# Attention heads of a hybrid decoder layer: sample rows in array tiles, group weights on turned probabilities, features stored by class

## The chip, the cores and the metric

The program runs on one core of one Trainium2 chip. The metric is the device time of one execution in microseconds (us). TensorE (PE in the profile) multiplies matrices into PSUM, VectorE (DVE), ScalarE (ACT) and GpSimd (POOL) work elementwise, and SyncE (SP) issues most transfers.

## The reference

One layer of a hybrid decoder runs for a prompt of 1024 tokens and for 8 sample sequences of 8 new tokens (64 sample rows). After an RMSNorm one combined projection gives the inputs of three branches: dilated window attention, a gated linear recurrence (HGRN2) and causal pooling. Each branch is gated, projected and merged, and an output projection follows. The attention is the part that changes:

```python
A_PATTERNS = ((128, 1), (512, 4), (2048, 16))      # (window, dilation) of the 3 groups, 4 heads x 128 each
def dilated_attn_sample(q, k_all, v_all, dilation, n_steps):
    idx = (n_ctx - T + jnp.arange(T))[:, None] - dilation * jnp.arange(n_steps + 1)[None, :]
    scores = jnp.einsum('bthe,btjhe->bthj', q, k_all[:, idx_c], ...) * (e ** -0.5)
    scores = jnp.where(valid[None, :, None, :], scores, NEG)
    lse = jax.nn.logsumexp(scores, axis=-1)
    p = jnp.exp(scores - lse[..., None])
    o = jnp.einsum('bthj,btjhe->bthe', p, vg)
...
w_grp = jax.nn.softmax(jnp.stack(lses, axis=0), axis=0)      # weight of each group, per token and head
o_a = jnp.einsum('gblh,gblhe->blhe', w_grp, jnp.stack(outs, axis=0))
y_a = (o_a * jax.nn.silu(ag))
```

For the prompt, token t of a group with dilation d reads keys t - j*d, so tokens fall into residue classes modulo d. The last 128, 512 and 1024 key and value rows of the three groups are outputs too. In the recurrence branch each of 8 heads also has 8 sample states of 128x128, read and updated by the sample rows.

## The kernel before, in words

The program is a sequence of phases: norm, attention (4 heads, one loop turn each), recurrence (`hgrn_phase`, 8 heads), pooling, two merges, output. All share a *conveyor*: a weight tile of 1024x128 is loaded by SP (`cv.load`, two slots), split by POOL into a high and a low part, and projected by PE in three token chunks (384, 384, 320 columns) of 24 matmuls each (`cv.project`, L230). ACT copies every chunk out of PSUM banks 0 to 2. The other PSUM banks form a ring of 3 in attention (banks 3, 4, 7): `cv.fill` lets PE write a ring bank once DVE has copied out the use three before, `cv.filled` lets DVE read it. Uses of the ring are numbered within a head (`M_S`, `M_K`, `M_V`, `M_KT`, ...), and every engine works strictly in its written order.

One attention head projects 10 units: queries and keys of the three groups (units 0 to 5), values (6 to 8) and the gate (9). Unit 0 belongs to the end of the previous turn. PE's order in a turn is: units 1, 2; prompt scores of group 0 (L1350); key rows of group 0 turned from features to rows for the key output (L1361); units 3, 4; the same for group 1; units 5, 6; the same for group 2. Then the cached sample keys, four 128-row blocks for each of the 8 sequences, are turned (`keys_t`, L1386), and the sample scores are made (`key_scores`, L1394) with the keys as the stationary operand and 8 query columns as the moving one. They lie under the chunks of units 7 and 8, together with the value rows (`v_rows`). The scores are copied out by DVE and turned back to rows (L1431). Unit 9 follows, then the sample probabilities are turned, and `sample_values` (L1458) multiplies them with the cached values, in 32 matmuls of 64 columns of probability that are zero outside the own sequence. At last the 35 probability blocks of the prompt are turned four at a time (`turn`, L1473), copied by DVE (L1721), and multiplied with the value rows (`values`, L1483 to L1491).

An fp32 matmul shows as two records in the trace. Features of a token stand in the order of time, so that groups 1 and 2 read them with a step of 4 or 8 elements:

```python
if g == 1:
    r, n = c // 2, c % 2
    return src[:, 4 * P * n + r:4 * P * n + r + 4 * (P - 1) + 1:4]
return src[:, c:c + 8 * (P - 1) + 1:8]
```

The group weights need all three groups' row maxima and sums by token. After ACT's exponentials (`exps(2)`, L1525), SP writes the statistics of groups 1 and 2 to HBM (L1296, L1299), waits for them, reads them back by token (L1303), DVE works out the weights (L1669 to L1684, with one exponential on ACT between), and SP carries them back by class (L1309 to L1317). DVE then scales all 24 pieces of the probabilities (L1704) before PE may turn them (`scaled`).

In `hgrn_phase`, `own_states` (L896 to L904) multiplies the queries of the 64 sample rows with the 8 sample states (8 matmuls, queries zero outside the own sequence) and makes the 8 state updates in two matmuls of 512 columns.

Of the kernel before, what the change touches and what calls it, by code (L numbers as in the profile page):

```python
# [25 lines left out]
F32 = mybir.dt.float32  # L26
F32R = mybir.dt.float32r
I32 = mybir.dt.int32
ALU = mybir.AluOpType
# [4 lines left out]
P = 128  # L34
# [30 lines left out]
def constants(np):  # L65
# [15 lines left out]
    c["level"] = lev  # L81
    j = np.arange(NS)
# [23 lines left out]
def build(nc, A, OUT):  # L106
    ctx = ExitStack()
    with ctx:
# [31 lines left out]
        weight_d = nc.dram_tensor("group_weights", (AH, SEQ, 2), F32, kind="Internal").ap()  # L140
# [544 lines left out]
        def hgrn_phase(ext, p_gate, p_graw, then):  # L685
# [10 lines left out]
            with scope:  # L696
# [71 lines left out]
                with nc.Block() as block:  # L768
# [86 lines left out]
                    def _(pe):  # L855
# [29 lines left out]
                        def own_states(i):  # L885
                            cv.copied(pe, i * MISC, M["k"] + 2)
                            for q in range(2):
                                bank = cv.fill(pe, i * MISC, M["ds"] + q)
                                for b in range(4):
# [7 lines left out]
                                      start=True, stop=False)  # L897
                            for b in range(NB):
                                mm = pe.matmul(bank[0:NS, 0:P], qown[:, b, :], s0[:, b, :],
                                               start=False, stop=(b == NB - 1))  # L900
# [229 lines left out]
        def attention_phase(then):  # L1130
# [7 lines left out]
            UNITS, MISC = 10, 51  # L1138
            KB = 4
            KW = KB * P + AG * NS  # L1140
            K_G = (0, 1, 1, 2)
            scope = ExitStack()
            with scope:
# [25 lines left out]
                wt = sb("a_weight", (P, TILES, 2), F32, scope)  # L1169
                w0 = sb("a_weight0", (P, TILES), F32, scope)  # L1170
                w12 = sb("a_weight12", (P, 2, TILES), F32, scope)
                yt = graw

                kv = [sb(f"s_cached{i}", (P, KB, P), F32, scope) for i in range(NB + 4)]
                VC = [8, 9, 10, 11, 0, 1, 2, 3]
                mask = sb("s_mask", (NS, KW), F32, scope)
                qh = sb("s_q", (P, AG, NS), F32, scope)
                kh = sb("s_k", (P, AG, NS), F32, scope)
                kt = [sb(f"s_k_feature{i}", (P, KB, P), F32, scope) for i in range(2)]
                sct = sb("s_scores_t", (P, KB, NS), F32, scope)  # L1180
# [5 lines left out]
                orow = sb("s_o_rows", (NS, P), F32, scope)  # L1186
                s_rows_ready = sem("s_rows_ready", scope)
                s_turned = sem("s_turned", scope)
# [8 lines left out]
                s_scores_out = sem("s_scores_copied", scope)  # L1197
# [6 lines left out]
                scores_max = sem("a_negmax_ready", scope)  # L1204
                exp_done = sem("a_exp_done", scope)
# [6 lines left out]
                weights_in = sem("a_weights_in", scope)  # L1212
                scaled = sem("a_prob_scaled", scope)
                krow_ready = sem("a_krow_ready", scope)
                krow_out = sem("a_krow_out", scope)
                vrow_out = sem("a_vrow_out", scope)
                o_done = sem("a_o_done", scope)
# [3 lines left out]
                CHAIN = 52  # L1221
# [13 lines left out]
                def tokens(src, g, c):  # L1235

                    if g == 0:
                        return src[:, c * P:(c + 1) * P]
                    if g == 1:
                        r, n = c // 2, c % 2  # L1240
                        return src[:, 4 * P * n + r:4 * P * n + r + 4 * (P - 1) + 1:4]
                    return src[:, c:c + 8 * (P - 1) + 1:8]

                def keys(src, g, c):
                    if g == 0 and c > 0:
                        return src[:, (c - 1) * P:(c + 1) * P]
                    if g == 1 and c % 2 == 1:
                        return src[:, c // 2:c // 2 + 4 * (2 * P - 1) + 1:4]
# [866 lines left out]
```

## Time and profile before

| | |
|---|---|
| time, median of 3 runs | 2058.72 us (2058.25 to 2058.84) |
| the profiled execution's own time | 2058.29 us |
| its span | 2056.5 us |
| PE busy | 1975.0 us, 96% |
| DVE, ACT, POOL busy | 761.6, 350.0, 472.0 us |
| mean granted clock of PE | 0.985 |

The span is what the profile shows from the first to the last instruction; 1.8 us of the execution lie around it. A matmul's duration in the trace contains its way through the array, so the distance between the starts of two records is what one costs in a dense stream. "PEclk" is the granted share of 2.4 GHz.

### The profile page before, as it was taken

Reading aid. Unit: us, or ns where it says so; the run is one execution under the profiler, and the core shown is the slowest. Engines: PE = TensorE matmul, PEld = TensorE weight load, DVE = VectorE, ACT = ScalarE, POOL = GpSimd, SP = SyncE. Lnnn points to the kernel's source line nnn. Section 1 sums busy time; section 2 is a strip of 40 time slices with the busy share of each in tenths; the row PEclk is TensorE's granted clock in tenths of the full one; section 3 lists DMA queues with packets and bytes.
Section 4 is the critical chain, followed back from the end, with each engine's and each line's share of the span. In section 5 each row is a group of like instructions: output and inputs, shape, how many; then the busy total and the mean of one; then the engine's idle time right before and its main releaser. Section 6 shows DMA issues by size and latency. Waiting matters only on the chain. (4 is left out here: it accounts for less than half of the span.)

```text
span 2056.5 us, 35111 instructions
## 1 busy us (share of the span) xinstructions
PE 1975.0 (96%) x13768; PEld 1906.1 (93%) x13768; DVE 761.6 (37%) x1378; ACT 350.0 (17%) x795; POOL 472.0 (23%) x276
## 2 busy tenths in 40 slices
PE   6999999999999999999999999999899999999796
PEld 6999999999999999999999999988899999999796
DVE  5224214222412425456556645636300132222423
ACT  5111121012112201110110111111211121111221
POOL 2211121121112112122111212222333333333220
PEclk8999999999999999999999999999999999999898
DMA  4313312222231221211111221112521132222612
GB/s 148 108 47 69 98 45 66 70 84 58 51 104 49 51 69 52 64 36 56 54 49 45 63 63 36 58 55 86 177 73 62 65 117 79 78 78 74 219 31 87
DMA packets 243967, 152.88 MB, mean 74 GB/s; under 512 B 34861, under 2 KB 231853, under 8 KB 243884
## 3 DMA queue, kind: packets, MB, share of 16 engines
q1 hardware_dynamic: 206012, 117.85, 19.6%
q10 hardware_dynamic: 37872, 33.79, 5.0%
q8 instruction: 68, 1.11, 0.2%
q14 instruction: 15, 0.12, 0.0%
HBM read 117.19 MB, written 34.42 MB: 74 GB/s over the span
## 5 line engine op out<-in xcount | busy, mean ns | idle before, releaser
L230 PE MATMUL psum<-x_hi,w_hi 128*128 128x384 f32 (+1 forms) x2688 | 888.9, 335 | 24.4 <-DVE x_lo L2026 10.5
L230 PE MATMUL psum<-x_lo,w_hi 128*128 128x384 f32 (+1 forms) x2688 | 870.2, 328 | 0.0
L230 PEld LDWEIGHTS psum<-x_hi,w_hi 128*128 128x128 f32 x2688 | 509.2, 189 | 41.4 <-issue 24.4
L230 PEld LDWEIGHTS psum<-x_lo,w_hi 128*128 128x128 f32 x2688 | 510.0, 190 | 0.0
L230 PE MATMUL psum<-x_hi,w_lo 128*128 128x384 f32 (+1 forms) x2688 | 498.1, 326 | 0.0
L204 POOL CAST w_hi<-w_raw 128x1024 fp32r<-128x1024 f32 (+1 forms) x136 | 140.9, 1036 | 1530.9 <-PE psum L230 1248.1
L230 PEld LDWEIGHTS psum<-x_hi,w_lo 128*128 128x128 f32 x2688 | 451.5, 188 | 0.0
L206 POOL TENSOR_TENSOR w_lo<-w_raw,w_hi 128x1024 fp32r<-128x1024 f32 (+1 forms) x136 | 330.9, 2433 | 10.9
L244 ACT ACTIVATE a_feature<-psum 128x384 f32<-128x384 f32 (+1 forms) x108 | 50.5, 473 | 390.1 <-PE psum L230 389.9
L244 ACT ACTIVATE c_ext<-psum 128x384 f32<-128x384 f32 (+1 forms) x96 | 45.1, 473 | 243.2 <-PE psum L230 234.2
L656 DVE TENSOR_TENSOR c_ext<-c_ext,c_gate 128x1088 f32<-128x1088 f32 x12 | 19.0, 1586 | 177.1 <-ACT c_ext L244 177.1
L656 DVE TENSOR_TENSOR c_ext<-c_ext,c_gate_raw 128x1088 f32<-128x1088 f32 x12 | 18.6, 1553 | 177.0 <-ACT c_ext L244 177.0
L230 PE MATMUL psum<-mb_y_hi,w_hi 128*128 128x384 f32 (+1 forms) x192 | 62.2, 329 | 2.4 <-DVE mb_y_lo L680 2.4
L1603 DVE COPY s_q<-a_feature 128x64 f32<-128x64 f32 x12 | 9.0, 748 | 148.0 <-ACT a_feature L244 148.0
L872 PEld LDWEIGHTS psum<-b_q_decayed,b_k_decayed 128*64 128x64 f32 x1584 | 51.3, 138 | 12.9 <-issue 8.4
L230 PE MATMUL psum<-mac_y_lo,w_hi 128*128 128x384 f32 (+1 forms) x192 | 62.4, 329 | 0.0
L230 PE MATMUL psum<-mb_y_lo,w_hi 128*128 128x384 f32 (+1 forms) x192 | 62.3, 329 | 0.0
L230 PE MATMUL psum<-mac_y_hi,w_hi 128*128 128x384 f32 (+1 forms) x192 | 62.3, 328 | 0.0
L1610 DVE TENSOR_TENSOR a_prob<-psum,band 128x128 f32<-128x128 f32 (+1 forms) x64 | 21.5, 377 | 103.7 <-PE psum L1350 102.8
L1013 DVE COPY_PREDICATED b_att<-b_level,psum 64x256 f32<-64x256 int32 (+2 forms) x136 | 58.8, 432 | 2.3
L872 PE MATMUL psum<-b_q_decayed,b_k_decayed 128*64 128x32 f32 x1584 | 56.6, 224 | 0.7
L1350 PE MATMUL psum<-a_feature 128*128 128x128 f32 (+1 forms) x192 | 52.9, 439 | 0.0
(214 smaller groups left out, 1940.6 us busy)
## 6 DMA issues: line engine op xcount, KB each, us to landing
w_raw<-in_w_in SPq DMA_DIRECT2D x104, 512.0 KB, 3.9
s_cached<-in_cache_kv_w SPq DMA_DIRECT2D x128, 64.0 KB, 2.5
s_cached<-in_cache_kv_w SPq DMA_DIRECT2D x64, 128.0 KB, 2.4
merged_rows<-c_ext ACTq DMA_DIRECT2D x15, 544.0 KB, 2.7
spare<-branch_outputs SPq DMA_DIRECT2D x10, 544.0 KB, 5.8
branch_outputs<-b_gate ACTq DMA_DIRECT2D x8, 544.0 KB, 3.2
c_ext<-merged_rows SPq DMA_DIRECT2D x8, 544.0 KB, 3.7
xt<-in_x_prompt SPq DMA_DIRECT2D x8, 512.0 KB, 8.8
```

What stands on the lines that cost most here:

```text
L204: pool.tensor_copy(w_hi[:, s, 0:nko, :], w_raw[:, s, 0:nko, :]).then_inc(self.hi_ready, 1)
L206: pool.tensor_tensor(w_lo[:, s, 0:nko, :], w_raw[:, s, 0:nko, :], w_hi[:, s, 0:nko, :].bitcast(F32), ALU.subtract)\
L230: mm = pe.matmul(psum[:, c, 0:n], w[:, s, k, :], x[:, k, t0:t0 + n], start=step is first, stop=step is last)
L244: act.activation(dst[:, t0:t0 + n], psum[:, c, 0:n], func).then_inc(self.bank_free, 1)
L656: ins = dve.tensor_tensor(pb[p][:, :], pb[p][:, :], gt[p][:, :], ALU.mult)
L872: mm = pe.matmul(bank[r:r + HP, b * wq:(b + 1) * wq], kr[:, t0 + r:t0 + r + HP], second(q[:, t0 + r:t0 + r + HP], n), start=True, stop=True)
L1013: ins = dve.copy_predicated(dst, msk, src)
L1350: mm = pe.matmul(bank[:, a:a + w], tokens(DST[U_Q[g]], g, c), keys(DST[U_K[g]], g, c), start=True, stop=True)
L1603: ch.step(dve.tensor_copy(dst[:, g, :], src[:, SEQ:NT]))
L1610: ins = dve.tensor_tensor(prob[:, a:a + w], ps_, mask, ALU.add)
```

## The change

**Features by class.** ACT copies each projected chunk of a query, key or value unit into its residue class order (step 1, 4 or 8), so `tokens` and `keys` read contiguous columns. The sample columns go to tiles of their own (`qh`, `kh`), and the queries also into `qown`, 32 columns per sequence that are zero outside the own 8. DVE's copies to `qh` and `kh` go.

**Fewer key rows.** Only the rows that are outputs are turned: 1 of 8 tiles in group 0, 4 in group 1, all in group 2, each with the sample rows.

**Sample scores.** The 32 query columns of a sequence are stationary and its turned keys move. Sequences b and b+4 write partitions 0 to 31 and 32 to 63. The scores come out as rows, so DVE's copy and PE's turn of them go.

**Sample values.** Products go to four 32-partition strips; a matmul with a constant `fold` adds and turns them at once. **Recurrence:** the sample outputs go to two strips, and each state update contracts over 32 rows only.

**Group weights.** They are written as three rows of 1024, read back to all partitions into freed feature tiles (3 transfers of 512 KB), and multiplied on while DVE copies the turned probabilities. The 24 scalings go. The probability blocks are regrouped, still 35 in 9 uses.

**Order.** The first chunk of unit 7 comes before `keys_t(0)`; `exps(2)` comes right behind it on ACT. DVE works out the weights after the fourth turned key block and before the fifth. SP's second load of the next turn's weights and the loads of the values of sequences 4 to 7 move behind the statistics.

```diff
+            for b in range(NB // 2):                                   # hgrn own_states
+                for r in range(0, NS, 4 * TB):
+                    br = b + r // TB
+                    mm = pe.matmul(bank[r:r + 4 * TB, 0:P], qown[:, br, r:r + 4 * TB], s0[:, br, :], ...)
+            banks = [cv.fill(pe, i * MISC, M["dss"] + q, True) for q in range(2)]
             for q in range(2):
-                bank = cv.fill(pe, i * MISC, M["dss"] + q, True)
-                pe.matmul(bank[:, :], krow[0:NS, TILES, :], vown[:, 4 * q:4 * q + 4, :],
+                r = 4 * TB * q
+                pe.matmul(banks[q][:, :], krow[r:r + 4 * TB, TILES, :],
+                          vown[r:r + 4 * TB, 4 * q:4 * q + 4, :],
...
-                M_S, M_K, M_V = (0, 7, 14), (4, 11, 18), (29, 34, 38)
-                M_KT, M_NEW, M_SC, M_SPT, M_O = 21, 32, 33, 37, 42
-                M_P = [41] + [43 + n for n in range(8)]
+                M_S, M_K, M_V = (0, 5, 11), (4, 9, 15), (24, 30, 34)
+                M_KT, M_NEW, M_SPT, M_O, M_BACK = [18 + n for n in range(6)] + [27, 28], 29, 33, 38, 39
+                M_P = [37] + [40 + n for n in range(8)]
...
                                                                        # SP
                             cv.load(sp, h * UNITS + UNITS, 0, after[0])
-                            sp.wait_ge(keys_used, h + 1)
-                            for b in range(4, NB):
-                                load_rows(sp, kv[VC[b]], b, 1, hd, v_in[b])
                             sp.wait_ge(exp_done, h * AG + AG)
...
                             sp.dma_start(comm[:, :, :, :], ...).then_inc(stats_in, 16)
-                            cv.load(sp, h * UNITS + (UNITS + 1), 1, after[1])
+                            sp.wait_ge(keys_used, h + 1)
+                            for b in range(4, NB):
+                                load_rows(sp, kv[VC[b]], b, 1, hd, v_in[b])
                             sp.wait_ge(weights_ready, h + 1)
+                            for g in range(AG):
+                                where = d[g].rearrange("(r b i) -> i r b", r=STEP[g], b=TILES)
+                                sp.dma_start(where, wt[:, :, g], ...).then_inc(weights_out, 16)
+                            sp.wait_ge(weights_out, h * 48 + 48)
+                            cv.copied(sp, h * MISC, M_V[0] + 2)
+                            for g in range(AG):
+                                if g == 2:
+                                    cv.copied(sp, h * MISC, M_V[1] + 2)
+                                sp.dma_start(spread_w[g], d[g:g + 1, :].broadcast_to([P, SEQ])).then_inc(weights_in[g], 16)
+                            cv.load(sp, h * UNITS + (UNITS + 1), 1, after[1])
...
                                                                        # PE
+                            def key_scores(i):
+                                cv.copied(pe, m0, M_KT[i + 1])
+                                for g, n0, n1 in ((0, 0, 1), (1, 1, 3), (2, 3, 4)):
+                                    for b in ORDER[i:i + 2]:
+                                        r = b // 4
+                                        mm = pe.matmul(psum[QB * r:QB * r + QB, 5, n0 * P:n1 * P],
+                                                       qown[:, g, b * QB:(b + 1) * QB], kt[r][:, n0:n1, :]...)
-                            pe.wait_ge(scores_max, h * AG + AG)
-                            pe.wait_ge(y_ready, h + 1)
+                            chunk(7, 0)
                             keys_t(0)
                             keys_t(1)
-                            chunk(7, 0)
+                            chunk(7, 1)
+                            pe.wait_ge(y_ready, h + 1)
                             key_scores(0)
-                            key_scores(1)
                             keys_t(2)
                             keys_t(3)
-                            chunk(7, 1)
-                            key_scores(2)
-                            key_scores(3).then_inc(keys_used, 1)
+                            chunk(7, 2)
+                            key_scores(2).then_inc(keys_used, 1)
                             keys_t(4)
                             keys_t(5)
-                            chunk(7, 2)
+                            v_rows(0)
+                            chunk(8, 0)
                             key_scores(4)
-                            key_scores(5)
                             keys_t(6)
                             keys_t(7)
-                            v_rows(0)
-                            chunk(8, 0)
-                            key_scores(6)
-                            key_scores(7).then_inc(s_scores_done, 1)
+                            chunk(8, 1)
+                            key_scores(6).then_inc(s_scores_done, 1)
...
+                                for b in range(NB // 2):                # sample_values
+                                    for n in range(2):
+                                        for quad in range(4):
+                                            br, nq = b + 4 * (quad % 2), n + 2 * (quad // 2)
+                                            a = (nq * NB + br) * NS + QB * (quad % 2)
+                                            mm = pe.matmul(bank[QB * quad:QB * (quad + 1), 0:P], own[:, a:a + QB],
+                                                           kv[VC[br]][:, nq, :], ...)
...
                                                                        # ACT
+                        act.wait_ge(q_own_clear, 1)
+                                ins = act.activation(by_class(DST[j][:, 0:SEQ], g)[:, :, t0 // STEP[g]:end // STEP[g]],
+                                                     psum[:, c, 0:end - t0].rearrange("p (m r) -> p r m", r=STEP[g]),
+                                                     ACT.Copy)
-                            unit(7)
+                            chunk(7, 0)
                             exps(2)
+                            chunk(7, 1)
+                            chunk(7, 2)
...
                                                                        # DVE
+                            for i in range(4):
+                                key_features(i)
                             dve.wait_ge(exp_done, h * AG + AG)
                             dve.wait_ge(stats_in, h * 16 + 16)
...
                             dve.sem_inc(weights_ready, 1)
+                            key_features(4)
+                            key_features(5)
+                            dve.wait_ge(vrow_out, h * V_OUT + V_OUT)
+                            rows(vrow[0], M_V[0])
+                            key_features(6)
+                            key_features(7)
...
-                                    ch.step(dve.tensor_scalar(prob[:, a:a + w], prob[:, a:a + w], sc, None, ALU.mult))
...
-                                dve.tensor_copy(pt[n % 2][:, 0:nb, :], bank[:, 0:nb * P]
+                                dve.tensor_tensor(pt[n % 2][:, 0:nb, :], bank[:, 0:nb * P]
+                                                  .rearrange("p (a b) -> p a b", b=P), token_weights(n), ALU.mult)\
```

## Rows read from the trace of the kernel before

**Rows 1.** Page, part 1: busy us, share of the span, instructions
```profile
PE 1975.0 (96%) x13768; PEld 1906.1 (93%) x13768; DVE 761.6 (37%) x1378; ACT 350.0 (17%) x795; POOL 472.0 (23%) x276
```

**Rows 2.** PE's waits, whole span: us in total, times, longest
```profile
PE psum L1386 <- DVE a_k_rows L1637: 7.0, 4, 1.8
...
PE psum L926 <- DVE b_o_rows L1114: 6.1, 7, 0.9
```

**Rows 3.** Timeline of PE, first head, prompt scores: start, duration, records (x)
```profile
68.37 3.41 PE L1350 MATMUL psum<-a_feature 128*128 128x128 f32 x16
71.62 1.04 PE L1361 MATMUL psum<-ident,a_feature 128*128 128x128 f32 x8
...
96.67 5.76 PE L1350 MATMUL psum<-a_feature 128*128 128x128 f32 x16
102.25 1.06 PE L1361 MATMUL psum<-ident,a_feature 128*128 128x128 f32 x8
...
127.17 4.07 PE L1350 MATMUL psum<-a_feature 128*128 128x128 f32 x16
131.06 1.05 PE L1361 MATMUL psum<-ident,a_feature 128*128 128x128 f32 x8
```

**Rows 4.** Timeline of PE, first head, one chunk, sample scores and values
```profile
134.99 0.42 PE L230 MATMUL psum<-x_hi,w_hi 128*128 128x384 f32 x1
...
139.26 1.84 PE L1394 MATMUL psum<-s_q,s_k_feature 128*128 128x8 f32 x16
140.97 1.07 PE L1386 MATMUL psum<-ident,s_cached 128*128 128x128 f32 x8
...
187.84 7.20 PE L1458 MATMUL psum<-s_cached,s_prob_t_own 128*64 128x128 f32 x64
194.97 0.44 PE L230 MATMUL psum<-x_hi,w_hi 128*128 128x384 f32 x1
```

**Rows 5.** Timeline of PE, first recurrence head: two-tile and one-tile products, own states
```profile
792.64 1.26 PE L872 MATMUL psum<-b_q_new,b_k_decayed 128*64 128x64 f32 x34
...
818.15 1.15 PE L867 MATMUL psum<-b_q_decayed,b_k_decayed 128*64 128x64 f32 x16
...
828.15 1.96 PE L899 MATMUL psum<-b_sample_state,b_q_own 128*64 128x128 f32 x16
830.04 1.98 PE L904 MATMUL psum<-b_v_own,b_k_rows 64*128 64x512 f32 x4
831.95 0.45 PE L230 MATMUL psum<-x_hi,w_hi 128*128 128x384 f32 x1
```

**Rows 6.** Timeline of DVE, first head: maxima, weights
```profile
133.05 0.17 DVE L1630 TENSOR_SCALAR a_stats<-a_max 128x8 f32<-128x8 f32 x1
...
166.16 0.17 DVE L1669 TENSOR_TENSOR a_least<-a_stats,a_stats_by_token 128x8 f32<-128x8 f32 x1 [2.72 <-DMA a_stats_by_token<-stat_rows]
...
168.34 0.24 DVE L1684 TENSOR_TENSOR a_weight<-a_group_exp,a_denominator 128x8 f32<-128x8 f32 x2
```

**Rows 7.** Timeline of ACT, first head: the first and the last of the eight exponentials
```profile
152.70 0.39 ACT L1525 ACTIVATE a_prob<-a_prob,a_stats 128x128 f32<-128x128 f32 x1
...
155.69 0.19 ACT L1525 ACTIVATION_READ_ACCUMULATOR a_prob<-a_prob,a_stats 128x1 f32 x1
```

**Rows 8.** Timeline of SP, first head: the read of the statistics
```profile
163.87 0.40 SPq L1303 DMA_DIRECT2D a_stats_by_token<-stat_rows  x1
```

**Rows 9.** Stretch of PE in head three: length, busy (records), granted clock, DMA share, GB/s
```profile
487.90:491.10 3.20, 3.20 (x13) 0.50 0.07 22
```

**Rows 10.** Groups by form, DVE and ACT: count, busy us, mean ns
```profile
L1721 DVE COPY a_prob_t<-psum 128x512 f32<-128x512 f32 x32 | 22.1, 691 | 17.3 <-PE psum L1473 16.8
...
L1689 DVE TENSOR_TENSOR s_prob<-psum,s_mask 64x512 f32<-64x512 f32 x4 | 2.7, 682 | 0.9 <-DVE a_weight L1684 0.9
...
L244 ACT ACTIVATE a_feature<-psum 128x384 f32<-128x384 f32 x72 | 34.8, 491 | 274.3 <-PE psum L230 274.0 <-issue 0.2
```

**Rows 11.** Timeline of DVE, start of the attention phase
```profile
41.33 1.82 DVE L1593 MEMSET s_prob_t_own<- 128x2112 f32 x1 [5.67 <-PEq L354]
```

More of the change, by code:

```diff
@@ L81, in constants @@
     c["level"] = lev
+    c["fold"] = np.tile(np.eye(NS, dtype=np.float32), (P // NS, 1))
     j = np.arange(NS)
@@ L1211, in attention_phase @@
                 weights_out = sem("a_weights_out", scope)
[L1212 to L1213 removed]
+                weights_in = [sem(f"a_weights_in{g}", scope) for g in range(AG)]
                 krow_ready = sem("a_krow_ready", scope)
@@ L1259, in attention_phase, with token_weights @@
+                BLOCKS += [[(1, c, T_AT[1][c], c - 1) for c in range(1, TILES, 2)]]
+                BLOCKS += [[(2, c, T_AT[2][c], c) for c in range(4 * n, 4 * n + 4)] for n in range(2)]
+                N_PT = len(BLOCKS)
                 assert N_PT == len(M_P)
+                def token_weights(n):
+                    g, c0, nb = BLOCKS[n][0][0], BLOCKS[n][0][1], len(BLOCKS[n])
+                    step = BLOCKS[n][1][1] - c0
+                    return spread_w[g].rearrange("p (c i) -> p c i", i=P)[:, c0:c0 + step * (nb - 1) + 1:step, :]
@@ L1379, in _, with keys_t @@
                             scores(2)
-                            rows(DST[U_K[2]], M_K[2], 0)
-                            def keys_t(b):
+                            k_rows(2)
+                            def keys_t(i):
+                                b = ORDER[i]
                                 pe.wait_ge(k_in[b], h * 48 + 48)
-                                bank = cv.fill(pe, m0, M_KT + b)
+                                bank = cv.fill(pe, m0, M_KT[i])
                                 for n in range(KB):
@@ L1425, in _ @@
                                                start=True, stop=True)
-                            mm.then_inc(cv.misc_done, 1)
-                            chunk(8, 1)
-                            pe.wait_ge(s_scores_out, h + 1)
-                            bank = cv.fill(pe, m0, M_SC, True)
-                            for n in range(KB):
-                                mm = pe.transpose(bank[0:NS, n * P:(n + 1) * P], sct[:, n, :], ident[:, :])
                             mm.then_inc(cv.misc_done, 1)
@@ L1452, in sample_values @@
                                     pe.matmul(bank[0:NS, 0:P], spt[:, g, :], vrow[g][0:NS, TILES, :],
-                                              start=(g == 0), stop=False)
-                                for b in range(NB):
-                                    pe.wait_ge(v_in[b], h * 48 + 48)
-                                    for n in range(KB):
-                                        a = (n * NB + b) * NS
-                                        mm = pe.matmul(bank[0:NS, 0:P], own[:, a:a + NS], kv[VC[b]][:, n, :],
-                                                       start=False, stop=(b == NB - 1 and n == KB - 1))
+                                              start=(g == 0), stop=False, skip_group_check=True)
@@ L1647, in _ @@
-                            rows(krow, M_K[1])
+                            k_rows(1)
                             scores(2)
-                            dve.wait_ge(krow_out, h * 96 + 96)
-                            rows(krow, M_K[2])
-                            for b in range(NB):
-                                bank = cv.filled(dve, m0, M_KT + b)
-                                dve.tensor_copy(kt[b % 2][:, :, :], bank.rearrange("p (a b) -> p a b", b=P))\
-                                    .then_inc(cv.misc_free, 1)
```

241 lines of the change are left out of this document (132 added, 109 removed).

## The prediction

> **What bounds the kernel.** I read the busy shares first: PE is busy 96% of the span and the next engine 37% [rows 1], so PE's own instructions and the few places where it waits set the time. I read PE's waits next. In attention there is one that this change touches: 7.0 us in four heads, at the first turned key block, for DVE's copy of key rows; in the recurrence PE waits up to 0.9 us a head for DVE's output rows [rows 2]. The timelines of PE, head by head, then give the price of each piece: what counts is the distance between starts. The lines of DVE, ACT and SP matter only for new waits.
>
> **Prompt scores.** Group 0 reads whole rows: its 16 records (2 of 128 columns, 14 of 256) take 71.62 - 68.37 = 3.25 us. Group 1, step 4, has 8 of 128 and 8 of 256 and takes 102.25 - 96.67 = 5.58 us; group 2, step 8, has 16 of 128 and takes 131.06 - 127.17 = 3.89 us, 0.243 each [rows 3]. Unstepped, a record of 128 columns costs 0.109 us (1.74 us for 16, from the 7.13 us of 64 records in the sample values less their start [rows 4]), so one of 256 costs (3.25 - 0.22) / 14 = 0.217. Contiguous, group 1 takes 8 x 0.109 + 8 x 0.217 = 2.61 and group 2 takes 1.74. Gain: 2.97 + 2.15 = 5.1 us a head. The Trainium skill (SBUF — State Buffer, "Door 1: The DMA port swizzle") says a step of up to four fp32 elements is free; the step-4 row, twice as long as contiguous reading, disagrees. By that rule group 1 would gain nothing and the total below would be 12 us smaller.
>
> **Key rows.** 7 turned tiles fewer in group 0 and 4 in group 1: 11 x 0.109 = 1.2 us a head. DVE's smaller copies lie under the projections.
>
> **The wait at the first turned key block.** Now a chunk of projection, 139.26 - 134.99 = 4.2 us [rows 4], stands between the group 2 key rows and `keys_t(0)`, more than the 1.75 us that PE waited on average [rows 2]. Gain: 1.75 us a head.
>
> **Sample scores.** Before, two sequences cost 140.97 - 139.26 = 1.70 us (16 records, stationary operand of 128 columns, only 8 columns moving) [rows 4]. Now they are 12 records in two 32-column strips: 8 of 128 and 4 of 256 moving columns, 8 x 0.109 + 4 x 0.217 = 1.74 us if one after another. But strips run side by side here: 34 records alternating over two 64-column strips take 793.83 - 792.64 = 1.19 us, 0.035 each, and 16 of the same shape in one strip take 1.07 us, 0.067 each [rows 5]. So half of 1.74, 0.87, plus some 0.2 for going to another tiling and back (the four L904 records, 512 columns, take 1.91 us where 4 x 0.427 is 1.71 [rows 5]): 1.1 us. Gain 0.6 x 4 pairs = 2.4 us a head; bounds 2.4 and -1.0 (no overlap). The turn of the scores goes as well: 4 records of 0.109 less the start, 0.35 us.
>
> **Sample values.** 64 records now take 194.97 - 187.84 = 7.13 us [rows 4]. After: as many, over four strips. The trace has no row with four. The two-strip row bounds it above at 64 x 0.055 + 0.2 = 3.7 us, full overlap below at 16 x 0.109 + 0.2 = 2.0 us. In the two-strip row records start in pairs from the first one on, so strips don't wait for the other half of an fp32 product; I take 2.0. Gain: 5.1 us a head; bounds 5.1 and 0.
>
> **Price of nothing.** DVE's product into `pt` costs what the copy cost: PSUM times SBUF over 512 columns 0.68 us against 0.69 [rows 10], and PE works 12 x 0.109 = 1.3 us per use. The 24 scalings lie under unit 9, and they don't appear among PE's waits. ACT's copies with steps may go from 0.49 to, as bound, twice that [rows 10]; a bank has two other chunks, some 7.7 us, before it is needed. The three weight rows are 3072 pieces of 4 bytes; 2048 pieces of 8 bytes took 8.0 us from ACT's last exponential to their landing [rows 7, 8], so 12 us in proportion. They are issued some 26 us after the end of unit 6 and needed at 57. The second weight load lands some 48 us after it, before the slot's unit 9 is even projected (53). The fold matmul replaces a turn of the same size. `qown`'s clearing, 768 of the 2112 columns that took 1.82 us, delays ACT's first copies by 0.65 to 0.9 us, once [rows 11]: I take 0.9.
>
> Sum in attention: 5.1 + 1.2 + 1.75 + 2.4 + 0.35 + 5.1 = 15.9 us a head, 63.6 in four.
>
> **A new wait.** DVE now waits for the statistics between the fourth and fifth key block, and the turned block in front of it holds a bank of the ring. `v_rows(0)` is uses 24 to 26; the second needs use 22, the fifth key block, copied. Count from T, the end of unit 6 (127.17 in the first head before [rows 3]). PE: scores and key rows to T+2.95, chunk (4.15) T+7.1, `keys_t` x2 T+7.95, chunk T+12.1, scores T+13.2, `keys_t` x2 T+14.1, chunk of 320 columns (3.5) T+17.7, scores T+18.8, `keys_t` x2 T+19.7, first four value tiles T+20.2. The statistics: DVE's maxima are ready before the chunk (133.2, T+6, even before [rows 6]), ACT copies the chunk by T+7.8 and needs 155.88 - 152.70 = 3.2 for `exps(2)` [rows 7]: T+11.0. From that end to DVE's first weight operation passed 166.16 - 155.88 = 10.3 us (8.0 of it two small writes to HBM [rows 7, 8]), DVE's weights take 168.58 - 166.16 = 2.4 more [rows 6] and the copy of the key block 0.7 [rows 10]: T+24.4. PE waits 24.4 - 20.2 = 4.2 us a head. Queued behind it on PE are unit 8 and all that follows; nothing else can fill it. If the writes are quicker without the twelve loads that stood before them, a microsecond or so less; bounds 2.5 and 6. That is -16.8 in four heads.
>
> **The clock.** Behind this phase's old wait, in the third head, the granted clock was 0.50 for 3.4 us [rows 9], the level of 1.2 GHz; the same wait in the other heads brought none. A hole twice as long brings it more often: I take three of four, 1.7 us each, less the one that goes: -3.4. Bounds 0 and -6.8.
>
> **Recurrence.** `own_states`: 16 records in two strips, 8 x 0.109 + 0.2 = 1.1 for 1.89 us; the state updates, 1.91 us, would take 1.1 if two row strips overlap, 1.9 if not [rows 5]. No row shows row strips; I take the middle, 1.5. Gain 1.2 a head, 9.6 in eight; bounds 12.8 and 0. DVE's chain to the output rows begins with PE's outputs, so its 0.9 us wait moves along unchanged.
>
> Total: 63.6 - 16.8 - 3.4 + 9.6 - 0.9 = 52.1 us, from the profiled execution's 2058.3 (median 2058.7): **2006.5 us**.
>
> **Rivals.**
> *Four strips go at the pace of two* (chance 0.2): sample values cost 1.7 us more a head, 2013. The Trainium skill (TensorE: Matmul & The Clock Gate, "The mechanism") says matmuls start and end in program order; by that rule the second half of a product holds up the next strip, and this rival is what comes out.
> *Narrow strips don't overlap* (0.08): sample values +5.1, two of the four score pairs +0.9 each (the first two only shorten the wait), recurrence +1.2 x 8: 4 x 6.9 + 9.6 = 37, so 2043. Against it: the two-strip row. For it: strips of 32 columns are not in the trace.
> *The statistics come in time* (0.1): no wait, no clock loss: 2006.5 - 16.8 - 5 = 1985. It would need HBM writes 4 us shorter, half of what they took in each head.
> *The wait is longer* (0.12): three new things share DVE and SP; at 8 us a head, 2022.
> *Slower than before* (0.04): a hole of 4 us puts the clock at half, and the strips, sparse in columns, keep it there to unit 9. That stretch is 16.4 us a head at full clock, so it costs 65.6 us, less the 5 already counted: 2067. It decides from 13 us of full-clock work a head at half. Against: dense projection ended such a stretch after 3.4 us [rows 9].
> *The forecast* (0.46), with its own range 1999 to 2013.
>
> Range 1988 to 2028: only the no-wait case, most of it, and the no-overlap and clock cases are outside. A measurement of this kernel can tell 0.2%, 4 us, from no change. Faster 0.94, same 0.02, slower 0.04.
>
> **What would show it.** Groups 1 and 2 of L1350 near 2.6 and 1.75 us; score pairs at 1.1 us; sample values at 2.0 (or 3.7, 7.1); a PE hole of some 4 us a head in front of the second value span, released by DVE's copy of the fifth key block, with the clock at 0.50 behind it; the turn-and-multiply pace still 1.33 us. A hole in front of the first weighted `pt` use, or ACT copies on PE's waits, would prove me wrong.

## The result, and the profile after

The changed kernel takes 2003.7 us (median of 4 runs, 2001.0 to 2005.6) beside 2058.8 for the kernel before in the same session: ratio 0.9722, 95% interval 0.9709 to 0.9736. The forecast was 2006.5. The profiled execution took 2004.9 us, of which the span is 2003.1 (mean granted clock 0.979, 0.985 before).

Part 1 of the page of the kernel after, to be held against [rows 1]:

```profile
PE 1906.1 (95%) x13648; PEld 1840.0 (92%) x13648; DVE 722.0 (36%) x1247; ACT 354.9 (18%) x855; POOL 472.2 (24%) x276
```

PE still sets the time: 69 us less work, and a smaller share of a span that is 53 us shorter, so part of the gain went into waiting. PE's waits (total, times, longest) name the place in their first line:

```profile
PE psum L1372 <- DVE s_k_feature L1712: 20.8, 4, 5.9
```

The wait at the first turned key block [rows 2] is gone; one of 5.2 us a head stands in `v_rows` (L1372). The recurrence's wait is the same as in [rows 2], 6.1 us. PE's timeline of the first attention head shows the new prices, first the prompt scores:

```profile
97.10 2.78 PE L1361 MATMUL psum<-a_feature 128*128 128x128 f32 x16
99.72 0.60 PE L1384 MATMUL psum<-ident,a_feature 128*128 128x128 f32 x4
...
123.97 1.95 PE L1361 MATMUL psum<-a_feature 128*128 128x128 f32 x16
125.75 1.04 PE L1372 MATMUL psum<-ident,a_feature 128*128 128x128 f32 x8
```

From start to start, group 1 takes 2.62 us and group 2 takes 1.78, where it was 5.58 and 3.89 [rows 3]. Then the sample scores, the hole, and what PE did behind it:

```profile
136.12 1.06 PE L1424 MATMUL psum<-s_k_feature,s_q_own 128*32 128x128 f32 x12
137.12 1.09 PE L1414 MATMUL psum<-ident,s_cached 128*128 128x128 f32 x8
...
143.57 0.60 PE L1372 MATMUL psum<-ident,a_feature 128*128 128x128 f32 x4
149.47 1.12 PE L1372 MATMUL psum<-ident,a_feature 128*128 128x128 f32 x4 [5.30 <-DVE s_k_feature L1712]
150.46 0.67 PE L231 MATMUL psum<-x_hi,w_hi 128*128 128x384 f32 x1
150.92 0.52 PE L231 MATMUL psum<-x_lo,w_hi 128*128 128x384 f32 x1
```

A score pair takes 1.00 us (1.70 before [rows 4]). The first four value tiles are done, and the next four start 5.3 us late. Projection records behind the hole start 0.32 us apart where 0.17 to 0.18 is usual: half clock. Four stretches, one behind the hole of each head (columns as in [rows 9]), show that it comes every time. A fifth, from the first head, shows that the clock was already down before PE had anything to do again (the 2.1 us just before 147.2 still have 1.00):

```profile
149.47:153.90 4.43, 4.42 (x16) 0.50 0.48 83
316.87:321.20 4.33, 4.33 (x16) 0.50 0.56 102
482.58:488.40 5.82, 5.82 (x20) 0.50 0.50 86
649.97:655.70 5.73, 5.73 (x20) 0.50 0.93 59
147.30:149.40 2.10, 0.00 (x0) 0.50 0.55 156
```

Clock 0.50 is the level of 1.2 GHz. PE worked 20.3 us at that level. What this costs is best seen against experiment 1, which has no hole: the 50 records from the fifth value tile on take 7.3 us there in every head, and 9.1, 9.0, 9.7 and 9.7 us here, so 8.3 us were lost in four heads. Last, the sample values and, in the first recurrence head, the own states and state updates:

```profile
184.64 1.95 PE L1483 MATMUL psum<-s_cached,s_prob_t_own 128*32 128x128 f32 x64
186.52 0.44 PE L231 MATMUL psum<-x_hi,w_hi 128*128 128x384 f32 x1
...
788.35 1.07 PE L902 MATMUL psum<-b_sample_state,b_q_own 128*32 128x128 f32 x16
789.35 1.13 PE L908 MATMUL psum<-b_v_own,b_k_rows 32*128 32x512 f32 x4
790.40 0.45 PE L231 MATMUL psum<-x_hi,w_hi 128*128 128x384 f32 x1
```

64 records in 1.88 us (7.13 before [rows 4]); own states 1.00 and updates 1.05 (1.89 and 1.91 [rows 5]).

Who PE waited for is read from DVE and SP. DVE's timeline:

```profile
146.09 0.17 DVE L1728 TENSOR_TENSOR a_least<-a_stats,a_stats_by_token 128x8 f32<-128x8 f32 x1 [6.99 <-DMA a_stats_by_token<-stat_rows]
...
148.73 1.29 DVE L1712 COPY s_k_feature<-psum 128x512 f32<-128x512 f32 x2 [0.22 <-DVE a_weight L1742]
```

and SP's:

```profile
134.98 0.77 SPq L1300 DMA_DIRECT2D stat_rows<-a_stats  x1
...
142.27 0.41 SPq L1307 DMA_DIRECT2D a_stats_by_token<-stat_rows  x1
...
151.40 2.14 SPq L1319 DMA_DIRECT2D group_weights<-a_weight  x3
167.82 2.55 SPq L1328 DMA_DIRECT2D a_feature<-group_weights  x3
```

DVE sits idle for 7.0 us with a full bank of keys in front of it, because its next instruction needs the statistics, which go to HBM (134.98 to 142.27) and back (to 146.09). PE is two steps behind: it needs the ring bank that DVE would free.

Where the time went: the recurrence begins 39.8 us earlier (its first own states start at 788.4 beside 828.1), and eight recurrence heads are 14.0 us shorter. The rest of the span is as before.

### The profile page after: what moved, and what is told of

Its sections match the earlier page's. It is cut to its first block and busy times, and to the rows that moved or that the text cites. A ratio compares the mean times of both kernels' runs of the same rounds, so it can differ in the third digit from the quotient of the medians.

```text
span 2003.1 us, 34765 instructions
## 1 busy us (share of the span) xinstructions
PE 1906.1 (95%) x13648; PEld 1840.0 (92%) x13648; DVE 722.0 (36%) x1247; ACT 354.9 (18%) x855; POOL 472.2 (24%) x276
## 5 line engine op out<-in xcount | busy, mean ns | idle before, releaser
L245 ACT ACTIVATE c_gate<-psum 128x384 f32<-128x384 f32 (+1 forms) x48 | 22.4, 475 | 136.0 <-PE psum L231 81.2
L1578 ACT ACTIVATE a_prob<-a_prob,a_stats 128x128 f32<-128x128 f32 (+1 forms) x96 | 41.8, 444 | 0.0
```

The lines of the kernel that those rows point to most:

```text
L245: act.activation(dst[:, t0:t0 + n], psum[:, c, 0:n], func).then_inc(self.bank_free, 1)
L1578: ins = act.activation(prob[:, a:a + w], prob[:, a:a + w], ACT.Exp, bias=st[:, g, c, 0:1], scale=SCALE, accum_out=st[:, g, c, 1:2])
```

## The experiments

All are variants of the kernel after, or of an earlier experiment where the text says so. The numbers are ratios to the kernel before in the same session; 0.001 is 2.06 us. The kernel after has 0.9722. It was not timed again in the sessions of the experiments, so a difference to it is given as a span where the ratios and the medians differ.

**1. DVE's weights moved behind the value rows.** Four lines go ahead of the block that works out the weights, nothing else:

```diff
+                            key_features(4)
+                            key_features(5)
+                            dve.wait_ge(vrow_out, h * V_OUT + V_OUT)
+                            rows(vrow[0], M_V[0])
                             dve.wait_ge(exp_done, h * AG + AG)
                             dve.wait_ge(stats_in, h * 16 + 16)
...                                                        # DVE: weights, weights_ready
-                            key_features(4)
-                            key_features(5)
-                            dve.wait_ge(vrow_out, h * V_OUT + V_OUT)
-                            rows(vrow[0], M_V[0])
```

> The changed kernel, with DVE's wait for the statistics and its weight operations moved behind the fifth and sixth key block and the first value rows. Theory (the hole in front of the second span of value rows, 5.2 us a head on average in the profile of after, and the half clock behind it, some 2 us a head, come from this order alone): the hole is gone, four heads give 29 us, near 1975 us, and the granted clock in the attention heads stays at 1.00 behind the place. Rival 1 (weights then come too late): the group weights are written 3 us later; if their way to the chip takes over 30 us PE waits at the first weighted use and the gain is some 10 us or less. Rival 2 (the hole's clock loss is not the hole's): only 21 us.

Measured: 1976.7 us, 0.9583 (0.9552 to 0.9615), clock 0.986. PE's timeline has no hole and no half clock where they were (granted clock 1.00 from 140 to 160):

```profile
143.10 1.17 PE L1372 MATMUL psum<-ident,a_feature 128*128 128x128 f32 x8
144.43 0.44 PE L231 MATMUL psum<-x_hi,w_hi 128*128 128x384 f32 x1
```

and DVE's first weight operation waits, in this head, no longer for the transfer but only for DVE's own copy. Over four heads it waits 1.3 us for the transfer, where it was 27.0:

```profile
145.86 0.17 DVE L1732 TENSOR_TENSOR a_least<-a_stats,a_stats_by_token 128x8 f32<-128x8 f32 x1 [0.33 <-DVE a_v_rows L1686]
```

The hole and its half clock are DVE's order and cost 27 to 29 us of the kernel after.

**2. Sample values strip after strip.** The same 64 records, all of one strip before the next:

```diff
-                                for b in range(NB // 2):
-                                    for n in range(2):
-                                        for quad in range(4):
+                                for quad in range(4):
+                                    for b in range(NB // 2):
+                                        for n in range(2):
```

> The changed kernel, with the 32 sample value products in the order of the strips (8 of strip 0, then 8 of strip 1, ...) where the changed kernel goes round the four strips. Same products, same sum. Theory (a product waits only for its own strip, but PE looks only a few instructions ahead, so neighbours in the order must be of different strips): the 1.88 us of after become 7.1 us, four heads cost 21 us, near 2025 us. Rival (each strip has a deep queue of its own): no change, 2004 us.

Measured: 2020.4 us, 0.9794 (0.9762 to 0.9826), 15 to 17 us slower than the kernel after, where 21 were expected. The edit also puts the waits for the values of all eight sequences ahead of the first product; PE's timeline shows no idle time from them. The timeline:

```profile
183.80 5.95 PE L1483 MATMUL psum<-s_cached,s_prob_t_own 128*32 128x128 f32 x64
189.68 0.44 PE L231 MATMUL psum<-x_hi,w_hi 128*128 128x384 f32 x1
```

5.88 us for what takes 1.88 in turn, so the factor three of the whole gain is overlap of strips. It isn't the 7.0 of 64 records of 0.109: at each of the three changes of strip, the first four records of the new one start beside the last four of the old. At the first change the old ones start at 185.13, 185.24, 185.35 and 185.46, the new ones at 185.14, 185.27, 185.38 and 185.49. PE here looks some four records ahead.

**3. Features stored in time order, read with steps.** `by_class` keeps the order of time, and `tokens` and `keys` read with steps of 4 and 8 as before the change; the rest stays:

```diff
-                    return x.rearrange("p (r m) -> p r m", r=STEP[g])
+                    return x.rearrange("p (r m) -> p r m", r=1)
...
+                        return src[:, 4 * P * n + r:4 * P * n + r + 4 * (P - 1) + 1:4]
+                    return src[:, c:c + 8 * (P - 1) + 1:8]
```

> The changed kernel, with the features in the order of time again: ACT copies without a step, PE reads groups 1 and 2 with steps of 4 and 8. Theory (PE reads a stepped operand at half speed): scores of group 1 go from 2.6 to 5.6 us, of group 2 from 1.8 to 3.9, value rows of both by some 0.3, so 5.4 us a head, 21 us in all, near 2025 us. Rival (the new hole swallows part, since it lies behind them): below 10 us; against it the statistics are late by as much as the scores.

Measured: 2022.7 us, 0.9805 (0.9772 to 0.9837), 17 to 19 us slower than the kernel after, where 21 were expected. PE's timeline for group 2 is again that of [rows 3]:

```profile
125.06 4.06 PE L1370 MATMUL psum<-a_feature 128*128 128x128 f32 x16
128.95 1.06 PE L1381 MATMUL psum<-ident,a_feature 128*128 128x128 f32 x8
```

The turns beside the scores show which operand it is. In a turn the features are the stationary operand and the identity moves, and the 8 turns of value rows take 0.89 us from start to start here (128.95 to 129.84) and 0.87 in the kernel after (125.75 to 126.62). So a step costs when the moving operand has it; the 0.3 us a head that were expected from the turns did not come.

ACT's copies by form, in the kernel after (count, busy us, mean ns):

```profile
L1556 ACT ACTIVATE a_feature<-psum 128x384 f32<-128x384 f32 x72 | 35.2, 490 | 272.0 <-PE psum L231 272.0
```

490 ns with steps of up to 8 in PSUM, 491 in this experiment, without them: the reordering costs ACT nothing.

**4. Recurrence as before.** Own states over 64 columns in one strip, and each update contracting over all 64 rows (`krow[0:NS]` in place of `krow[r:r + 4 * TB]`).

> The changed kernel, with the own states of the recurrence as in the kernel before. Theory (strips overlap fully, by rows too): own outputs and updates take 3.8 us again instead of 2.05, 1.75 us in each of eight heads, 14 us, near 2018 us. Rival (part of it is given back at PE's wait for DVE's output rows): below 10 us.

Measured: 2019.2 us, 0.9784 (0.9752 to 0.9816). The timeline repeats [rows 5]:

```profile
790.92 1.96 PE L900 MATMUL psum<-b_sample_state,b_q_own 128*64 128x128 f32 x16
792.81 1.98 PE L905 MATMUL psum<-b_v_own,b_k_rows 64*128 64x512 f32 x4
794.72 0.45 PE L231 MATMUL psum<-x_hi,w_hi 128*128 128x384 f32 x1
```

3.80 us against 2.05, times eight is 14.0; the medians differ by 15.4.

**5. Work put into the hole.**

```diff
+                                    if m == M_V[0] and q == 0:
+                                        for _ in range(40):
+                                            pe.transpose(bank[:, 0:P], tokens(src, 0), ident[:, :])
```

> The kernel after, with 40 further turns of 128 columns (40 x 0.109 = 4.4 us of PE work a head at full clock) in the middle of the value rows of unit 6, in the same bank and right ahead of the span that waits for DVE; their result is written over by the span. Theory (the wait of some 5 us a head is for the statistics, and the half clock behind it comes from the idle time, not from the work): the added work fills the hole, costs nothing itself, and what the half clock took, about 2 us a head, comes back: near 1996. Rival A (the half clock behind the hole has another cause, such as what PE executes there): the time stays at 2004. Rival B (PE is what is late there and the wait is only shown at the wrong place): plus 4 x 4.4, near 2021.

Measured: 1995.8 us, 0.9682 (0.9664 to 0.9699), 8 us faster than the kernel after with 160 matmuls more. PE's timeline:

```profile
144.35 4.53 PE L1370 MATMUL psum<-ident,a_feature 128*128 128x128 f32 x40
...
150.19 0.66 PE L1375 MATMUL psum<-ident,a_feature 128*128 128x128 f32 x4 [0.88 <-DVE s_k_feature L1715]
...
151.01 0.44 PE L231 MATMUL psum<-x_hi,w_hi 128*128 128x384 f32 x1
151.29 0.34 PE L231 MATMUL psum<-x_lo,w_hi 128*128 128x384 f32 x1
```

Of the wait 0.9 us is left in this head and 3.3 of 20.8 us in all four, the granted clock is 1.00 from 143 to 155, the next value tiles start 0.7 us later than in the kernel after, and two records of projection take 0.28 us from start to start where half clock had 0.46. This splits the 28 us of experiment 1: some 8 are the half clock that follows idle time, the remaining 20 are the wait.

**6. Twelve loads moved away from the statistics' way.** SP issues the value loads of sequences 4 to 7 behind the weights' reads.

> The kernel after, with the twelve loads of the values of sequences 4 to 7, which SP issues right behind the read-back of the statistics, moved behind the weights' reads. Theory (the twelve loads share the DMA queues with the small pieces of the read-back, which took 3.8 us from issue to DVE against 2.3 in the kernel before): the read-back gets 1 to 1.5 us shorter and so does the hole in four heads: 1998 to 2000. Rival (the read-back's length has nothing to do with the loads): 2004. If the values now come late for the sample values, PE waits there, and the time is above 2004.

Measured: 2003.4 us, 0.9718 (0.9700 to 0.9735): no difference. SP issues the read-back at 141.66, and DVE starts at 145.21 (its timeline):

```profile
145.21 0.17 DVE L1727 TENSOR_TENSOR a_least<-a_stats,a_stats_by_token 128x8 f32<-128x8 f32 x1 [6.72 <-DMA a_stats_by_token<-stat_rows]
```

3.55 us in place of 3.82, but 2.29 before the change [rows 6, 8]. Over four heads the read-back takes 3.4 us with and without the loads behind it, and 2.3 before the change; the theory fell.

The traces show another transfer beside it, which this experiment left in place. ACT issues the 512 KB of group 2's key rows to HBM 0.1 to 1.1 us ahead of the read-back in the four heads of the kernel after. In the kernel before it issued them during `exps(2)`, some 10 us ahead of the read-back, and they had landed before that began; now `exps(2)` comes first. ACT's timeline of the kernel after, then the stretch of the read-back (columns as in [rows 9]) in the kernel before, the kernel after and this experiment:

```profile
141.90 0.59 ACTq L1593 DMA_DIRECT2D out_kv_p<-a_k_rows  x1
```

```profile
163.90:166.20 2.30, 2.30 (x15) 1.00 0.25 9
142.30:146.10 3.80, 1.88 (x18) 1.00 0.81 188
141.70:145.20 3.50, 1.86 (x18) 1.00 0.71 164
```

The DMA engines are 25% busy in the first stretch, 81% and 71% in the others. That write is the likely reason of the longer read-back; no run moves it, so this is not shown.

**7. Experiment 1, and the clearing waited for at its first use.**

```diff
-                        act.wait_ge(q_own_clear, 1)
                         with act.Fori(0, AH) as h:
...
                                     if j in U_Q:
                                         for r in range(2):
+                                            act.wait_ge(q_own_clear, 1)
```

> The first experiment (the weights behind the value rows of unit 6, 1976.7 us) with one more edit: ACT waits for the cleared own-query tile at its first use, the sample columns of the first query unit, and not ahead of its first copy. Theory (the clearing holds ACT's first copies back, and PE's gap at the start of attention is 3.7 us against 2.9 before): 0.8 us less, 1976. Rival (the gap at the start is the gap of the ring of banks and the clearing has ended before): no difference. This is also the candidate for the fastest version.

Measured: 1975.1 us, 0.9582 (0.9565 to 0.9599). The times can't tell 0.8 us; PE's timelines at the start of attention can, experiment 1 first:

```profile
44.01 0.60 PE L231 MATMUL psum<-x_hi,w_hi 128*128 128x384 f32 x1 [3.35 <-ACT a_feature L1556]
```

```profile
42.23 0.45 PE L231 MATMUL psum<-x_hi,w_hi 128*128 128x384 f32 x1 [2.55 <-ACT a_feature L1555]
```

With experiments 1 and 10 this is the fastest version: 4.2% under the kernel before, 1.4% under the kernel after.

**8. The 24 scalings back.** DVE multiplies the probabilities again, behind the third group of value rows, each piece waiting for the one before, into a tile that nobody reads then.

> The kernel after, with DVE again multiplying all 24 pieces of the prompt's probabilities one after another behind the third group of value rows, each by its inverse sum, into a tile that nobody reads at that time (some 7 us of DVE work a head, as the 24 scalings were before). Theory (the scalings lay under the projection of unit 9, and taking them away gave nothing): 2004, within 2 us. Rival (they held back DVE's copies ahead of the sample values or the first turned blocks, so taking them away was part of the gain): slower by 1 to 7 us a head, 2008 to 2032.

Measured: 2003.6 us, 0.9721 (0.9704 to 0.9739). Putting the scalings back costs nothing, so taking them away gained nothing.

**9. Experiment 7, with the first two turned key blocks ahead of the chunk again.**

```diff
-                            chunk(7, 0)
                             keys_t(0)
                             keys_t(1)
+                            chunk(7, 0)
```

> The kernel of the seventh run (weights behind the value rows, clearing waited for late; 0.958 of before), with the first two turned key blocks ahead of the first chunk of unit 7 again, as before the change. Theory (the chunk covers DVE's late copy of the key rows, which PE waited 1.75 us a head for): the wait comes back at the first turned key block, 1.5 to 1.9 us in four heads, 6 to 8 us slower than the seventh run, 0.961 to 0.962 of before. Rival (with fewer key rows and no copies of the sample columns DVE is no longer late there): no wait, 0.958.

Measured: 1984.7 us, 0.9636 (0.9616 to 0.9656), 11 us slower than experiment 7 where 6 to 8 were expected. The wait is back in full:

```profile
PE psum L1414 <- DVE a_k_rows L1686: 7.1, 4, 1.8
```

What was missed is the clock. Stretches right behind the wait in the four heads:

```profile
126.58:130.50 3.92, 3.92 (x17) 0.56 0.35 106
290.00:294.20 4.20, 4.20 (x27) 1.00 0.37 108
451.60:455.50 3.90, 3.90 (x17) 0.60 0.39 115
615.00:618.80 3.80, 3.80 (x15) 0.55 0.29 87
```

Three of four waits of 1.77 us are followed by half clock, a loss of 1.7 + 1.6 + 1.7 = 5 us, and 7.1 + 5 = 12. In the kernel before it was one of four [rows 9]. The same execution has gaps of 0.9 to 1.5 us at the ends of the four heads with full clock behind them. So the clock behind a hole of this length goes either way. Behind one of 4.4 to 5.9 us it fell in all 28 cases: four heads each of the kernel after and of experiments 2, 3, 4, 6, 8 and 11.

**10. DVE's weights behind all eight key blocks.**

> The kernel after, with DVE's work on the group weights behind all eight turned key blocks (in the first experiment it stood behind the value rows, two key blocks earlier, with the way of the weights unchanged). Theory (the weights' way has slack of several us: they are needed at the first weighted turn): no hole and nothing late, as the first experiment, 0.958 of before. Rival (the slack is used up or DVE is now late for what stands behind, the sample scores): a wait at the sample probabilities or at the first weighted turn, 0.960 or more.

Measured: 1974.3 us, 0.9581 (0.9565 to 0.9598), no different from experiment 1. SP writes the weights 4.1 us later than in the kernel after and reads them back at 173.08; DVE's first product with them, at 178.73, waited for nothing (SP's timeline, then DVE's):

```profile
155.48 2.14 SPq L1319 DMA_DIRECT2D group_weights<-a_weight  x3
173.08 1.43 SPq L1328 DMA_DIRECT2D a_feature<-group_weights  x3
```

```profile
178.73 0.69 DVE L1783 TENSOR_TENSOR a_prob_t<-psum,a_feature 128x512 f32<-128x512 f32 x1
```

The weights have at least these 4 us of slack. A read takes 5.7 us to land (median of the page's issues), so there is hardly more.

**11. Sample values two strips at a time.** First strips 0 and 1 in turn, then 2 and 3.

> The kernel after, with the 64 records of the sample values in another order: all of strips 0 and 1 in turn, then all of strips 2 and 3, so that only two strips can run beside each other. Theory (strips overlap fully as far as the order lets them): twice the time of four, 2 x 16 x 0.109 = 3.5 us for 64 records against 1.88, plus 1.7 us a head, 6.8 in all: near 2010.5. Rival (two narrow strips already run as fast as four, so the bound is something else, such as the supply of weights or of moving columns): 2004.

Measured: 2010.5 us, 0.9757 (0.9740 to 0.9774), 7 us slower than the kernel after, as expected:

```profile
183.88 3.29 PE L1484 MATMUL psum<-s_cached,s_prob_t_own 128*32 128x128 f32 x64
187.10 0.44 PE L231 MATMUL psum<-x_hi,w_hi 128*128 128x384 f32 x1
```

3.22 us: one, two and four strips take 5.88, 3.22 and 1.88.

## Why the prediction was right, step by step

**Prompt scores, 5.1 us a head:** measured (5.58 - 2.62) + (3.89 - 1.78) = 5.07; by the median of experiment 3, 4.3 to 4.8. Contiguous reading is what gives it, and the Trainium skill's rule for a step of four elements (SBUF — State Buffer, "Door 1: The DMA port swizzle") doesn't hold for the moving fp32 operand of PE here: group 1 halved.

**Sample values, 5.1:** measured 7.13 - 1.88 = 5.25. The rival "at the pace of two" is what an order with two strips gives (3.22, experiment 11), not what four strips give. The Trainium skill (TensorE: Matmul & The Clock Gate, "The mechanism") has matmuls start and end in program order; that doesn't describe these records. Every 0.11 us one record of each of the four strips starts, some 7 ns apart, although each product is two records; and at a change of strip the first four records of the next strip start ahead of their turn (experiment 2).

**Sample scores, 2.4, and their turn, 0.35:** measured 0.70 a pair, 2.8; narrow strips cost less around the edges than the 0.2 us allowed.

**Key rows, 1.2, and the wait at the first turned key block, 1.75:** the wait went as said, and experiment 9 shows that the order did it, not DVE's smaller load. The key rows gave 1.75 where 1.2 was said: from the first turn to the next projection passed 1.23 and 1.12 us in groups 0 and 1 of the kernel before (71.62 and 102.25 [rows 3] to the next L230 record at 72.85 and 103.37), and 0.14 and 0.46 after. For the sample scores and the key rows no experiment takes the change back; their gains are read from the timelines alone.

**What was priced at nothing:** right for the scalings (experiment 8), the stepped copies (experiment 3) and DVE's product (0.69 us, as the copy [rows 10]). The weights' three writes took 16.1 us in the first head, from the first issue at 151.40 to the last landing at 167.51, where 12 had been worked out in proportion; 4 us or more of slack hid it (experiment 10). The clearing cost 0.8 us, for the reason given (experiment 7).

**The new wait, 4.2 us a head:** right in place and cause (experiments 1 and 5), 1.0 too small. ACT's last exponential ends at T+10.8 and not 11.0 (T, the end of unit 6, is 123.97 now). From there to DVE's first weight operation passed 146.09 - 134.75 = 11.3 us in place of 10.3. The two writes took 7.5 us for 8.0, the sign that the prediction had guessed, and the read-back 3.8 for 2.3. The loads behind it aren't the cause (experiment 6); ACT's 512 KB write beside it is the likely one, not tested.

**The clock, -3.4:** half clock came in all four heads, at 8.3 us less the 1.7 of before: -6.6. The step was mis-sized in both factors (three of four, and 1.7 each for 2.1).

**Recurrence, 9.6 in eight:** measured 1.75 a head, 14.0 (experiment 4: 13 to 15). Own states as said, 1.00. The middle taken for two row strips was wrong: two matmuls that contract over different 32 rows overlap, 1.05 us for 1.91.

The sum from the records: gains of 5.07 + 1.75 + 1.75 + 2.8 + 0.35 + 5.25 = 17.0 a head, 67.9 in four, and 14.0; losses 20.8, 6.6 and 0.8. That makes 53.7, measured 2058.3 - 2004.9 = 53.4. The forecast of 52.1 was near by luck in its sizes: 4.3 too little in attention and 4.4 in the recurrence stood against 4.0 in the wait and 3.2 in the clock. The mechanisms it named were all there; only for the row strips had it left open whether they overlap.

Two slips in its arithmetic carry no weight: 2058.3 - 52.1 is 2006.2 (2006.5 lies between this and 2006.6 from the median), and with the 5 us of clock already in the forecast, the case of a kernel no faster than before needs 14.3 us of work a head at half clock, not 13.

## What to carry to other kernels

This change won 82 us of PE's time and lost a third of that again: look where an engine that only frees buffers (DVE) has an instruction in its order that waits for a round trip through memory, and ask what stands behind it. Here the same instructions, moved behind five copies, made the kernel 1.4% faster. Idle time of the matmul engine can cost more than its length, because the clock can be down behind it (20.8 us of waiting cost 8.3 more); even work of no use, put into the hole, made the kernel faster. With small stationary operands, put consecutive matmuls on different strips of the array. When a transfer is on the critical path, look also at what other engines issue at that moment.

## What the runs showed of the hardware

- fp32 matmuls of 32 stationary columns on four column strips run fully beside each other: 64 records of 128 moving columns take 1.88 us, on two strips 3.22, one strip after another 5.88.
- Two row strips of 32 contracted rows overlap as well: 4 records of 512 columns take 1.05 us, with 64 rows 1.91.
- PE starts records of another strip up to some four places ahead of the order (experiment 2, at each change of strip).
- With a moving fp32 operand read at a step of 4 or 8 elements these matmuls take twice as long (1.78 to 3.89 us for 16 records at step 8); with such a step in the stationary operand alone 8 turns take 0.89 us for 0.87; ACT reading PSUM with such a step and writing contiguously takes 490 ns for 384 columns, as without.
- 3072 pieces of 4 bytes written to HBM in three transfers took 16.1 us from the first issue to the last landing (first head of the kernel after).
- A read-back of 16 KB takes 2.2 to 2.6 us in the four heads of the kernel before, with the DMA engines 24% to 32% busy, and 2.6 to 3.8 us in those of the kernel after, with 55% to 90%.
- Holes of 4.4 to 5.9 us on PE were followed by half clock in 28 cases of 28 (4.3 to 5.8 us of it in the kernel after, where the clock fell while PE was still idle), holes of 1.8 us in three of four in one kernel and one of four in another. In the first head of experiment 9 the clock fell 1.5 us after PE had started again.
